# Reordering the vector and scalar engines' streams around the feed-forward products of a five-block fp32 kernel

## The reference

```
def _swiglu(x, w_in, w_out):
    gu = x @ w_in
    return (jax.nn.silu(gu[..., :D_FF_2]) * gu[..., D_FF_2:]) @ w_out
...
        x = x + _swiglu(_rmsnorm(x, g_ffn[i]), w_ffn_in[i], w_ffn_out[i])
```

## Time and profile before

| | us |
|---|---|
| median of 3 runs (lowest 2981.86, highest 2983.13) | 2982.35 |
| the profiled execution | 2981.86 |
| its span, first to last instruction | 2980.1 |
| PE busy in the span | 2965.6 |
| PEld / DVE / ACT / POOL busy | 2658.2 / 2253.8 / 1461.9 / 58.4 |

### The profile page before, as it was taken

One profiled execution on the slowest core, in us unless ns is written; L12 is line 12 of the kernel. 1 busy time (PEld: TensorE's weight loads), 2 busy tenths in 40 slices (PEclk: granted clock), 3 DMA queues, 4 the chain that ended last, 5 costly groups with the idle time before them and its releaser, 6 DMA issues.

```text
span 2980.1 us, 48028 instructions
## 1 busy us (share of the span) xinstructions
PE 2965.6 (100%) x18813; PEld 2658.2 (89%) x18813; DVE 2253.8 (76%) x2773; ACT 1461.9 (49%) x2144; POOL 58.4 (2%) x148
## 2 busy tenths in 40 slices
PE   9999999999999999999999999999999999999998
PEld 8779999988889999878899998789999878899997
DVE  7979888566759887566598874658888567588884
ACT  4476555454345555444455553325555344355553
POOL 6100000000000000000000000000000000000000
PEclk9999999999999999999999999999999999999999
DMA  6122332332133333221333333223333222133322
GB/s 189 49 75 88 104 121 97 113 130 71 55 101 99 99 106 100 92 63 57 104 103 99 99 106 106 85 68 116 100 100 106 93 84 66 62 113 99 110 95 78
DMA packets 256696, 283.32 MB, mean 95 GB/s; under 512 B 11874, under 2 KB 229152, under 8 KB 256552
## 3 DMA queue, kind: packets, MB, share of 16 engines
q1 hardware_dynamic: 256440, 281.28, 29.3%
q10 hardware_dynamic: 112, 0.02, 0.0%
HBM read 279.16 MB, written 4.73 MB: 95 GB/s over the span
## 4 chain that ended last, share of the span: by engine, by line
PE 93%; DVE 4%; POOL 1%; issue 1%; ACT 1%; ACTq 0%; DVEq 0%; POOLq 0%
PE ps L2885 40%; PE ps L2510 14%; PE ps L2512 14%; PE ps L2511 14%; PE ps L3238 1%; PE ps L3239 1%; PE ps L3240 1%; PE ps L3145 1%; PE ps L3205 1%; PE ps L3184 1%; PE ps L3224 1%; PE ps L3226 1%; PE ps L3225 1%; PE ps L3074 1%; PE ps L3094 1%
## 5 line engine op out<-in xcount | busy, mean ns | idle before, releaser
L818 ACT ACTIVATE whi<-raw 128x2048 fp32r<-128x2048 f32 (+2 forms) x144 | 246.5, 1712 | 488.9 <-PE ps L2512 411.4
L1477 DVE TENSOR_TENSOR wlo<-raw,whi 128x2048 fp32r<-128x2048 f32 (+2 forms) x144 | 293.6, 2039 | 223.8 <-ACT whi L818 223.5
L2885 PE MATMUL ps<-th,wh 128*128 128x256 f32 x1600 | 454.4, 284 | 0.6 <-DVE wl L1563 0.5
L2885 PE MATMUL ps<-tl,wh 128*128 128x256 f32 x1600 | 453.5, 283 | 0.0
L2885 PE MATMUL ps<-th,wl 128*128 128x256 f32 x1600 | 453.4, 283 | 0.0
L2510 PE MATMUL ps<-hh,whi 128*128 128x512 f32 x896 | 357.6, 399 | 0.0
L2512 PE MATMUL ps<-hh,wlo 128*128 128x512 f32 x896 | 350.0, 391 | 0.0
L2511 PE MATMUL ps<-hl,whi 128*128 128x512 f32 x896 | 349.6, 390 | 0.0
L2885 PE MATMUL ps<-hh,wh 128*128 128x256 f32 x1200 | 340.5, 284 | 0.0
L2885 PE MATMUL ps<-hh,wl 128*128 128x256 f32 x1200 | 340.2, 283 | 0.0
L2885 PE MATMUL ps<-hl,wh 128*128 128x256 f32 x1200 | 340.2, 283 | 0.0
(11 more groups left out here) (513 smaller groups left out, 6701.0 us busy)
## 6 DMA issues: line engine op xcount, KB each, us to landing
raw<-in_w_ffn_in SPq DMA_DIRECT2D x88, 1024.0 KB, 5.1
raw<-in_w_in SPq DMA_DIRECT2D x59, 1024.0 KB, 5.3
raw<-in_w_ffn_out SPq DMA_DIRECT2D x40, 1024.0 KB, 5.0
raw<-in_w_o SPq DMA_DIRECT2D x32, 640.0 KB, 4.1
raw<-in_w_gate SPq DMA_DIRECT2D x11, 1024.0 KB, 5.3
raw<-in_w_up SPq DMA_DIRECT2D x11, 1024.0 KB, 5.3
raw<-in_w_down SPq DMA_DIRECT2D x10, 1024.0 KB, 5.0
raw<-in_w_mem_kv SPq DMA_DIRECT2D x8, 1024.0 KB, 5.5
```

Of the source, the lines that this page charges most:

```text
L818: a.activation(whi[:, slot, 0:n], raw[:, slot, 0:n], ACT.Copy).then_inc(hi_made, 1)
L1477: v.tensor_tensor(wlo[:, u % 2, 0:n], raw[:, u % 2, 0:n], whi[:, u % 2, 0:n].bitcast(F32), ALU.subtract).then_inc(lo_made, 1)
L2885: e = mm(bank(b, HALF), wgt[:, q, w], xx, start=start and k == 0 and m == 0, stop=k == KD // 2 - 1 and m == 2, skip_group_check=True)
```

## The change

The computation stays the same. Seven statements move, on two engines; PE, POOL and SP keep their order.

```
@@ ACT, swiglu: high parts for the down products
                 act_high(s, 20, 2, 10)
-                ahead(u0 + 22)
                 moving_high(s, 0)
                 moving_high(s, 2)
+                act.wait_ge(unit_used, u0 + 22)
                 act_high(s, 16, 4, 9)
+                ahead(u0 + 22)
                 moving_high(s, 1)
                 moving_high(s, 3)
@@ ACT, swiglu: end of the block
                 for d in range(7, 12):
-                    if d == 11 and s:
-                        residual(r + 1, range(4, 7))
                     if d >= 8:
                         ahead(u0 + 22, 0, 0, d)
...
-                    if d == 11 and not s:
+                    if d == 11:
                         residual(r + 1, range(4, 7))
@@ DVE, seven
+                if not last:
+                    odd_low(p, 1 - slot, 1 - j, form(4))
+                    sums_low(p, form(5))
                 if j and not (isinstance(i, int) and i == 0):
                     dve.wait_ge(acc_free, at_turn(i, 2, gc + 2))
                     v.tensor_tensor(tiles_of_pair(i), tiles_of_pair(i), rs2[:, :, :], ALU.mult).then_inc(act_scaled, 1)
-                if not last:
-                    odd_low(p, 1 - slot, 1 - j, form(4))
-                    sums_low(p, form(5))
@@ DVE, down_run (the two lines of run_t come from the end of swiglu, where they stood ahead of low(u0 + 23))
                 v.tensor_tensor(tiles_of_pair(10), tiles_of_pair(10), rs2[:, :, :], ALU.mult).then_inc(act_scaled, 1)
+                dve.wait_ge(act_scaled, SCALED * s + 7)
+                dve.wait_ge(product_done, PRODUCTS * s + 120)
+                v.tensor_tensor(run_t[0][:, :, :], run_half(0, 0), run_half(0, 1), ALU.subtract).then_inc(sum_made, 1)
+                v.tensor_tensor(run_t[2][:, :, :], run_half(1, 1), run_half(0, 1), ALU.subtract).then_inc(sum_made, 1)
...
                 tile_lows(20, 2)
-                low(u0 + 24)
-                dve.wait_ge(sum_made, SUMS * s + 68)
                 for k, t in enumerate((0, 2)):
                     moved_low(s, t, 21 + k)
                 dve.wait_ge(ffn_hi, FFN_HIS * s + 23)
                 tile_lows(16, 4)
-                low(u0 + 25)
+                low(u0 + 24)
+                dve.wait_ge(sum_made, SUMS * s + 68)
                 for k, t in enumerate((1, 3)):
                     moved_low(s, t, 24 + k)
...
                 v.tensor_tensor(actl[:, 9:16:2, :], actr[:, 9:16:2, :], odd_hi[:, :, :].bitcast(F32), ALU.subtract).then_inc(ffn_lo, 1)
+                low(u0 + 25)
                 dve.wait_ge(loaded[p], 16 * (first // 2 + 1))
```

More of the change, by code:

```diff
@@ L1839, in swiglu @@
                 tile_lows(2, 2)
[L1840 to L1843, removed]
                 low(u0 + 23)
```

## The result

The changed kernel took 3022.5 us in the median of 4 runs (3018.55, 3022.81, 3023.39, 3022.19) and the kernel before 2982.56 (2981.86 to 2983.13, 4 runs), a ratio of 1.0132 with a 95% interval of 1.0114 to 1.0149. It is slower, as forecast. The forecast was 3015.6 with a range of 3009 to 3022, so the median lies 6.9 above the forecast and just past the range's upper end. The profiled execution took 3019.11.

A forecast was written before the change was run, and what follows sets the result against it. PE, busy nearly throughout at full clock, was taken to bound the kernel, so its added waits count one for one. Terms 11.6 + 19.6 + 2.0 = 33.2 on 2981.86, adjusted 0.5 to the median, gave 3015.6; range 3009 to 3022.

The forecast's parts named there:

- What bounds the kernel; room against length: Everywhere: PE sets the pace; a moved DVE instruction costs what it exceeds its room, in the loop 1.13 against 0.96.
- Once or each turn: Loop: each turn loses 0.17 and none makes up for it, 7 x 0.17 = 1.19 per block.
- The spacing on DVE: DVE neighbours of 1024 without a wait start 1.13 apart, not the full 1.22; full durations would give about 42, not 33.
- The price of a deciding wait: From DVE's end to PE's start, where PE waits just there: 0.15.
- Loads: Down products: the load for u0 + 26 issued some 6.7 later, priced at nothing, up to 0.5 per block as upper bound.
- The sum: Loop and exit 11.6, down products 19.6, ends of blocks 2 to 4 2.0: 33.2 in all; whole-sum case 0.83.
- rival 4: PE's clock falls to half in the new waits at d = 3: up to 54 more, 3070; 0.09 with other ways.
- A slice of the granted clock below full: Sign in the new profile: any of the granted clock's slices below full would show the prediction wrong.
- PE's busy time: Sign in the new profile: busy time about as before, idle time up by 20 or more.
- Rival 1: Only one large part decides: 3010 if turns make up their 0.17, 2996 if down-product waits meet unseen room; chance 0.05.
- rival 2: Loop and down products: the moves are hidden by room behind L1563 and an idle DVE queue, 2982; chance 0.02.
- rival 3: Loop: faster, as low parts no longer stand behind the scaling; price 5 x 0.17 = 0.9, so 2981; chance 0.01.

The follow-up runs named there:

- between: Kernel before with the scaling in DVE's seven placed between odd_low and sums_low: 2986.4 us against 2982.43, ratio 1.0013.
- loop_only: Kernel before with only the edit in DVE's seven, the scaling moved behind sums_low: 2994.58 us against 2982.43, ratio 1.004.
- down_only: Kernel before with only the down-product edits (DVE's run_t and two low parts later, ACT's copy of u0 + 24 later): 3007.15 us, ratio 1.0077.
- again: The changed kernel, unaltered, timed once more against the kernel before: 3018.38 us in the median, ratio 1.012.
- in_the_gap: Kernel before with the loop-exit scaling behind turn 9's take_late and ACT's copy of tile 0 in an idle gap of turn 9: 2981.55 us against 2982.6.
- short_wait: Kernel before with the down-product edits, but u0 + 25's low part in time, leaving only the wait at d = 2: 2991.62 us against 2982.75.

## Why the prediction was right, and what it left out

**What bounds the kernel; room against length.** Right, and in each place to about 0.07: 0.173 per turn in four blocks against 0.17, 1.13 to 1.14 at the exit against 1.13, 1.63 at d = 2 against 1.56, 2.37 at d = 3 against 2.36, and 0.6 at the ends of blocks 2 to 4 against 0.67. Each part run alone gave its own share, and between showed the room itself.

**Once or each turn.** Each turn, as argued. The first block's turns lag by 0.24 (0.23 in loop_only) instead of 0.17; this costs 0.5 us in all, and why block 1 differs stays open.

**The spacing on DVE.** In the new order 1.13 separates again two neighbours of 1024 without a wait between them (1094.11 to 1095.25). With full durations in place of these distances the sum was 42 in place of 33; without the clock's share the change cost 34.1 (below). The measurement decides against that sum. The prediction held it up as what the Trainium skill says (VectorE: DVE Perf Modes, The DRAIN you can't avoid), and quoted it by half: the same paragraph says that a next operation which isn't held starts earlier, and with that the 1.13 at a duration of 1.22 agrees.

**The price of a deciding wait.** The prediction took 0.15 from DVE's end to PE's start and nothing more. At d = 2 PE starts only 0.05 behind DVE's end (1138.04 + 1.22 to 1139.31), but the second matmul comes 0.34 behind it instead of 0.23. At the exit the 0.15 was there, and 0.08 more on the second matmul (1097.22 to 1097.42). So a wait that decides costs 0.15 to 0.23, split over two matmuls. A wait that stood before had that cost already; a new one adds it. Of the 0.07 at d = 2, 0.03 is DVE's chain (11.42 against 11.39) and most of the rest these hundredths on the second matmul and the next. The turns' 0.28 that the prediction looked for came as 0.20 and 0.22, two distances in place of one.

**Loads.** Priced at nothing, and nothing it was: the lag between d = 3 and the end of the block is 0.0 in all five, but for the clock's 1.59.

**The sum, the step that was mis-sized.** The prediction's sum, 33.2, has no term for the clock: its range of 3009 to 3022 is that of a kernel at full clock, and the fall of the clock stands beside it as rival 4, as another case. The runs showed that the two come together: one fall in one block of five in each of the two profiled runs of this kernel, three in that of down_only. That rival was also priced far too high, at up to 10.9 per block, on the thought that d = 3 might run at half speed to its end. One fall costs 1.6, because full speed is back after 3.4 us.

The change's own terms are 34.1 by the table: 6.5 for the turns, 25.7 for the exit, d = 2 and d = 3, 1.9 for the ends of the blocks. That is 0.9 above the forecast's, and the lowest run, whose mean clock of 0.999 fits no fall, lies 34.2 above the kernel before (3016.95 against 2982.75). The first series' median lies 39.9 above its kernel before (3022.5 against 2982.56). The 5.8 that are left would be three to four falls at 1.6. That count is inferred from the time and the mean clock of 0.997; no run with so many was profiled for this kernel. So the terms were right to 1, but where the median lies in or beyond the range was left to chance: the forecast had 6.4 of room to the range's end, the terms were 0.9 larger and the clock took 5.8 in that series, and in the series of "again" it took less.

The trace agrees with the Trainium skill, TensorE: Matmul & The Clock Gate, Part 1, in that an idle PE is set to its lower level, yet a single wait of 1.63 was not enough in any of five blocks.

**Two signs were badly chosen.** "A slice of the granted clock below full" can't show a fall of 3.4 us in slices of 75; stretches of 4 us do. And PE's busy time was to stay as it was, but it rose by 13.9 (2965.6 to 2979.5), and its idle time by 23.4. Of the 13.9, 1.6 is the fall of the clock. Part of a wait lies under the record of the matmul before it, and a matmul that waited has a longer record itself (0.50 in place of 0.39): the busy time of PE is no measure of its work.

**The rivals.** Rival 1 is refuted by the parts alone, rival 2 by the same, rival 3 by the times; rival 4 is answered above. Rival 3's price, 0.9 for the waits at the exit, was near what in_the_gap won, 1.05, with another edit.

## What to carry to other kernels

Where one engine sets the pace, measure the room between the end of what it waits for and its own start, and compare it with the length of what is to be moved there: 1.13 into 0.96 costs 0.17, and in a loop whose turns hang on one another each turn pays. To take such a wait away, follow what stands behind the moved instruction on every engine it signals: two moves out of three only handed the wait on, and the third worked since a hole was long enough. If the matmul engine comes to wait for more than the 1.6 us that cost nothing extra here, give its clock a term of its own in the sum, with a count and a price (1.6 per fall here), and look for it in stretches of a few us and in the scatter of the runs.

## What the runs showed of the hardware

- PE's clock went to its lower level after a wait of 2.8 in 5 blocks of 5, after 3.95 in 5 of 5, after 1.63 alone in 0 of 5, and after 1.63 and 2.37 with 5.4 of work between in 1, 1 and 3 of 5. The lower level then lasted 3.41 us, once 6.83. It cost 1.4 to 1.7 us of time, and 3.0 that once. Which of five like blocks it hits is open.
- The fall need not come within the wait. In the changed kernel's trace four matmuls had started at the upper level's pace again before it came, 1.0 us behind the end of the wait (1147.12 to 1148.1).
- It makes a kernel with such waits scatter: down_only's five runs spread over 5.3 us, those of short_wait over 1.4 and those of the kernel before over 1.8 (17 runs).
- A matmul of 512 columns starts 0.23 behind the last at the upper level and 0.43 at the lower.
